# The down projection of the window pairs in seven products of half blocks

## The chip, the cores and the metric

The kernel runs on one core of a Trainium2 chip, in float32. Its time is device microseconds (us) of one execution; the median of several is compared. The engines are TensorE (PE; PEld is its weight load), VectorE (DVE), ScalarE (ACT), GpSimd (POOL) and SyncE (SP); SP and POOL here only issue DMAs.

## The reference

One encoder layer is applied with shared weights to 512 prompt tokens and 2048 sample tokens, model width 1024. The part that matters here is the feed-forward network at its end, with hidden width 2816:

```
h2 = rms(x, norm2_g)
g = silu(dwconv3(h2 @ ffn_w_gate) + bias)     # three taps along the tokens
x = x + (g * (h2 @ ffn_w_up)) @ ffn_w_down
```

Ahead of it stand a norm, an input projection, windowed attention beside a convolution of 31 taps, and an output projection.

## The kernel before, in words

Activations lie transposed, channels on the 128 partitions and tokens along the free axis. Each float32 product is three matmuls of split operands: a high part (ScalarE rounds a copy) and a low part (VectorE subtracts the high part from the raw values) of each operand, high x high, high x low and low x high.

**Slots.** The first part of the kernel is a list of 242 slots (`SLOT`): input projections A of five chunks of 512 tokens (14 slots each), output projections O, and gate, up and down of two plain windows of tokens (G, D). Each slot uses one weight tile of a ring of four, loaded by SP four slots ahead. The input and output projection weights are split once and stored in DRAM (`weight_scratch`); later chunks load them from there. Work of the other engines hangs on the slots in lists (`ACT_SIDE`, `DVE_SIDE`, `POOL_SIDE`), in the engine's own order. A table of room per slot (`ROOM`, `WORK`, `conv_room`) deals VectorE's convolution steps over the slots; the attention part loads `cat` tiles for each O phase.

**Products.** The rest of the tokens is done in two pairs of windows of 414 columns each, in a list of products `PROD`. A gate or up tile pair (two hidden tiles, a "row pair", 11 of them) times two windows is a 2 x 2 block product, computed with seven products (P1 to P7) of half blocks in place of eight: sums of weight quarters (S1 to S4, `part_sum`, line 1907) times sums of window quarters (T1 to T4). A group is one such seven: gate and up of a row pair are two groups. Each product is 4 x 3 = 12 matmuls (line 2354) and needs its weight part split by ScalarE (`part_high`, line 1447) and VectorE (`part_low`, line 1924), three products ahead (`LEAD`), with a ring of four high parts (`HI_RING`).

ScalarE copies three of the seven results out of PSUM, VectorE adds the others to them (`pair_add`), ScalarE and VectorE do the three taps and the swish, VectorE multiplies gate and up (`pair_product`), and the result is split into `mid2` (`pair_mid_high`, line 1520, `pair_mid_low`, line 1980).

**Down.** The down projection of the pairs isn't done by sevens: for each pass (`PASSES`: row pair 0 alone, then five passes of two row pairs) its products D (`pair_down`, line 2358) stand in `PROD` in one run behind one product of the next group, and after the last group of a pair. A D product uses one weight tile for both windows: 24 matmuls. Each of a pass's 16 outputs (8 tiles of model width x 2 windows) is copied from one of four PSUM banks into one of four `pair_y` buffers by ScalarE (`pair_y_copy`, line 1502), and POOL issues a DMA that adds it into `y` in DRAM (line 1176), where the residual already lies. ScalarE waits for a buffer's DMA before it writes it again, and TensorE waits for the copy before it writes the bank again. The weight tiles have a ring of four of their own (`DOWN_RING`), so in a run of D products the split is made one product ahead.

**Order.** For each index of `PROD` each engine has a list (`ACT_AT`, `DVE_AT`, `SP_AT`); an engine works its lists strictly in order and waits on semaphores. The windows of the second pair are loaded, summed and split in the last seven products ahead of it (`WINDOW_STEPS`).

## Time and profile before

| | us |
|---|---|
| median of 3 runs | 2594.53 (2594.07 to 2597.62) |
| profiled execution | 2595.2 |
| its span, first to last instruction | 2592.9 |
| TensorE busy | 2562.3 |
| VectorE busy | 1756.2 |
| ScalarE busy | 1338.4 |
| mean busy share of the DMA engines at 1485 to 2587 us (the pairs) | 0.48 |

The slots take the first 1485 us, the pairs the rest, with 5808 matmuls. Busy time counts matmuls whose modelled spans overlap; the pitch from one to the next is shorter than the duration of one. Shares of DMA are means over the 16 engines; the packets of two queues can overlap on one engine.

### The profile page before, as it was taken

To read this page: it belongs to the slowest core of one execution; us is meant where nothing else is said; L and a number is where in the kernel's file an instruction comes from. 1 tells how busy PE (TensorE), PEld (TensorE's weight loads), DVE (VectorE), ACT (ScalarE), POOL (GpSimd) and SP (SyncE) were. 2 spreads that over 40 slices of the span, in tenths; PEclk is the share of its full clock that TensorE was granted. 3 is DMA by queue.
4 is the path that set the end of the run, shared out by engine and by line. 5 is a ranking of instruction groups with operands and counts; after the bars stand their busy time and mean duration, and the time that the engine had idled before them with its cause. 6 is when DMAs were issued, how large, how long until landed. Compare 5 with 4: busy or idle time off the path is not lost. (4 is left out here: it accounts for less than half of the span.)

```text
span 2592.9 us, 35676 instructions
## 1 busy us (share of the span) xinstructions
PE 2562.3 (99%) x12927; PEld 2288.2 (88%) x12927; DVE 1756.2 (68%) x2908; ACT 1338.4 (52%) x2358; POOL 344.4 (13%) x500
## 2 busy tenths in 40 slices
PE   8999999999999999999999999999999999999998
PEld 6877777788878888888788999999999999999998
DVE  4766658887887697868883666547548754754753
ACT  6345444468337834683573455445445554544543
POOL 0110021101011111110101110120120122012012
PEclk9999999999999999999999999999999999999999
DMA  9967788734554375447439553562554555255254
GB/s 352 343 236 239 249 290 339 276 113 162 209 207 143 138 257 202 169 155 267 156 114 359 189 116 85 109 117 68 116 110 126 115 110 114 72 112 114 67 108 69
DMA packets 161214, 446.76 MB, mean 172 GB/s; under 512 B 27824, under 2 KB 60976, under 8 KB 144400
## 3 DMA queue, kind: packets, MB, share of 16 engines
q1 hardware_dynamic: 108208, 307.75, 34.3%
q0 software_dynamic: 52832, 136.72, 21.6%
q8 instruction: 104, 1.70, 0.3%
q14 instruction: 70, 0.57, 0.1%
HBM read 321.23 MB, written 123.17 MB: 171 GB/s over the span
## 5 line engine op out<-in xcount | busy, mean ns | idle before, releaser
L1930 DVE TENSOR_TENSOR part_lo<-part_raw,part_hi 128x512 fp32r<-128x512 f32 x396 | 271.2, 689 | 425.9 <-ACT part_hi L1462 421.8
L2208 PE MATMUL bank<-hw_hi,weights 128*128 128x462 f32 (+3 forms) x1408 | 420.6, 373 | 0.0
L1751 DVE SCALAR_TENSOR_TENSOR cc<-win,par,cc 128x512 f32<-128x512 f32 x600 | 408.2, 744 | 0.0
L2368 PE MATMUL bank<-mid,part_hi 128*128 128x414 f32 x1408 | 378.4, 349 | 6.9 <-ACT pair_y L1513 4.7
L2159 PE MATMUL bank<-h_hi,weights 128*128 128x512 f32 x1104 | 354.4, 394 | 0.0
L2208 PEld LDWEIGHTS bank<-hw_hi,weights 128*128 128x128 f32 x1408 | 264.7, 188 | 37.3 <-issue 12.2
L1176 POOL DMA_DIRECT2D y_t<-pair_y x192 | 163.4, 861 | 938.9 <-ACT pair_y L1513 936.6
L1462 ACT ACTIVATE part_hi<-part_raw 128x512 fp32r<-128x512 f32 x396 | 244.5, 624 | 81.7 <-PE bank L2354 81.6
L2368 PEld LDWEIGHTS bank<-mid,part_hi 128*128 128x128 f32 x1408 | 262.8, 188 | 12.1 <-ACT pair_y L1513 6.5
L2208 PE MATMUL bank<-hw_lo,weights 128*128 128x464 f32 (+3 forms) x704 | 259.2, 368 | 0.0
L2159 PEld LDWEIGHTS bank<-h_hi,weights 128*128 128x128 f32 x1104 | 207.2, 188 | 51.4 <-issue 5.9
L2354 PE MATMUL bank<-T_hi,part_hi 128*128 128x414 f32 (+1 forms) x704 | 246.2, 350 | 0.2 <-DVE e L1954 0.2
L2354 PE MATMUL bank<-T_lo,part_hi 128*128 128x414 f32 (+1 forms) x704 | 246.1, 350 | 0.0
L2354 PE MATMUL bank<-T_hi,part_lo 128*128 128x414 f32 (+1 forms) x704 | 245.8, 349 | 0.0
L2368 PE MATMUL bank<-mid,part_lo 128*128 128x414 f32 x704 | 245.1, 348 | 0.0
L1513 ACT ACTIVATE pair_y<-bank 128x414 f32<-128x414 f32 x192 | 99.2, 518 | 247.0 <-PE bank L2368 223.6
L1644 DVE TENSOR_TENSOR weights<-wraw,weights 128x1024 fp32r<-128x1024 f32 x154 | 187.9, 1220 | 55.3 <-ACT weights L1198 55.2
L2224 PE MATMUL bank<-mid,weights 128*128 128x462 f32 (+1 forms) x1056 | 223.9, 370 | 0.0
L2224 PEld LDWEIGHTS bank<-mid,weights 128*128 128x128 f32 x1056 | 197.0, 188 | 22.8 <-issue 5.0
L2159 PE MATMUL bank<-h_lo,weights 128*128 128x512 f32 x552 | 215.3, 390 | 0.0
L1198 ACT ACTIVATE weights<-wraw 128x1024 fp32r<-128x1024 f32 x154 | 162.9, 1058 | 91.7 <-DMA wraw<-w_down_t 65.7
L2193 PE MATMUL bank<-cat_hi,weights 128*128 128x512 f32 x640 | 205.2, 395 | 3.0 <-DMA cat_lo<-cat_scratch 3.0
(223 smaller groups left out, 4464.3 us busy)
## 6 DMA issues: line engine op xcount, KB each, us to landing
weights<-weight_scratch SPq DMA_DIRECT2D x88, 1024.0 KB, 6.5
wraw<-w_ffn_t SPq DMA_DIRECT2D x88, 512.0 KB, 3.5
part_raw<-w_ffn_t SPq DMA_DIRECT2D x176, 256.0 KB, 2.7
y_t<-pair_y POOLq DMA_DIRECT2D x192, 207.0 KB, 4.0
weight_scratch<-weights POOLq DMA_DIRECT2D x22, 1024.0 KB, 7.8
wraw<-w_down_t SPq DMA_DIRECT2D x44, 512.0 KB, 3.5
part_raw<-w_pass_t SPq DMA_DIRECT2D x88, 256.0 KB, 3.5
cat_hi<-cat_scratch SPq DMA_DIRECT2D x10, 1024.0 KB, 6.8
```

What stands on the lines that cost most here:

```text
L1176: pool.dma_start(y[o, :, window_start(w):window_start(w) + TP], y_out[n % 4][:], accum_op=ALU.add).then_inc(s_yadd[n % 4], 16)
L1198: nc.scalar.activation(whi[n % RING], wraw[n % RING][:], ACT.Copy).then_inc(s_whi, 1)
L1462: nc.scalar.activation(p_hi[k % HI_RING][:], p_raw[part_of(k)][:], ACT.Copy).then_inc(s_whi, 1)
L1644: nc.vector.tensor_tensor(wlo[n % RING], wraw[n % RING][:], whi[n % RING].bitcast(F32), ALU.subtract) \
L1751: nc.vector.scalar_tensor_tensor(acc, win[i][:, tap:tap + TB], w_tap, acc, ALU.mult, ALU.add).then_inc(s_cv, 1)
L1930: nc.vector.tensor_tensor(p_lo[part_of(k)][:], p_raw[part_of(k)][:], p_hi[k % HI_RING][:].bitcast(F32), ALU.subtract).then_inc(s_wlo, 1)
L2159: mm = nc.tensor.matmul(out[:], l[:, k, :], r[:, k, :], start=(k == 0 and i == 0), stop=(k == KT - 1 and i == 2))
L2193: mm = nc.tensor.matmul(out[:], l[:, k, :], r[:, k, :], start=(k == 0 and i == 0), stop=(k == KT - 1 and i == 2))
L2208: mm = nc.tensor.matmul(out, l[:, k, :], r[:, k, cols], start=(k == 0 and j == 0), stop=(k == KT - 1 and j == 2))
L2224: mm = nc.tensor.matmul(out, l[:, q, :], mid[:, k, part, 0:WIDTH[w]], start=(k == 0 and j == 0), stop=(k == FH - 1 and j == 2))
L2354: mm = nc.tensor.matmul(out, l[:, t, :], r[:, t, cols], start=(p in (1, 2, 5) and t == 0 and j == 0), stop=(t == KH - 1 and j == 2), skip_ ...
L2368: mm = nc.tensor.matmul(bank[BANK_Y[n % 4]][:, 0:TP], l[:, (deep * o + t) % KH, :], mid2[:, t, part, i, :], start=(t == 0 and z == 0), sto ...
```

## The change

- The down projection of the pairs becomes seven products too. A D product is now (pair, pass, product p, row pair): 4 outputs x 3 = 12 matmuls on one part of 256 KB. A pass has 7 phases, in the order 5, 3, 1, 6, 7, 4, 2; a phase has one D product per row pair of the pass. Phases 5, 1 and 2 begin their four banks anew, the others go on in what stands there, so that each phase leaves four results that belong to one of the four quarters of `y` (`DOWN_OUT`); they are copied and added into `y` after every phase, 28 per pass. The ring of `pair_y` buffers has six in place of four.
- Phases of a pass are dealt one by one behind the products of the next row pair, from P6 of its gate group to P4 in its up group. The last pass of a pair stays in one run behind the last group. The changed order of the last group (6, 2, 7, 3) goes.
- `mid2` holds seven tiles (B11, T1, T2, B21, B22, T3, T4) for two row pairs. VectorE makes four sums per row pair (`pair_mid_sum`), and seven tiles are split in place of four.
- The sums of down weights are made in the slots: at slots 12, 17, ..., 62 SP loads the four quarters of a row pair (1 MB), three slots later VectorE makes four sums, and one slot after that POOL stores all four tiles of 256 KB in DRAM (`down_sums`). The load of the next waits for the store of the last. `WORK` knows them, so the convolution steps are dealt anew.
- Some semaphores are shared by more loads (`residual_loaded`, `y_residual_loaded`), and tiles of the pairs lie elsewhere in SBUF.

The core of the diff:

```diff
+COMBO_AT = [12 + 5 * r for r in range(FT // 2)]
...
+for _r in range(FT // 2):
+    DVE_SIDE[COMBO_AT[_r] + 3].append(("combo", _r))
+    POOL_SIDE[COMBO_AT[_r] + 4].append(("combo", _r))
...
+DOWN_ORDER = (5, 3, 1, 6, 7, 4, 2)
+DOWN_FRESH = (5, 1, 2)
+DOWN_OUT = {1: (0, 0), 2: (0, 0), 3: (0, 1), 6: (0, 1), 5: (1, 1), 7: (1, 1), 4: (1, 0)}
+COMBO = {"A21": 0, "A22": 1, "A11": 2, "A12": 3, "S3": 0, "S1": 1, "S2": 2, "S4": 3}
+COMBO_SUMS = (("S1", "A21", "A22"), ("S3", "A21", "A11"), ("S2", "S1", "A11"), ("S4", "A12", "S2"))
...
 PROD = []
 for _q in range(PAIRS):
+    _behind = []
     for _i in range(ROW_PAIRS):
+        if _i > 0 and PASS_OF[_i] != PASS_OF[_i - 1]:
+            _behind = [[("D", _q, PASS_OF[_i - 1], _p, _r) for _r in PASSES[PASS_OF[_i - 1]]] for _p in DOWN_ORDER]
         for _s in range(2):
             _g = 2 * _i + _s
-            PROD += [("P", _q, _g, 1), ("P", _q, _g, 5)]
-            if _g > 0:
-                PROD.append(("P", _q, _g - 1, 4))
-            for _p in (6, 2, 7, 3) if ends_pair(_g) else (6, 2, 3, 7):
-                PROD.append(("P", _q, _g, _p))
-                if _s == 0 and _i > 0 and PASS_OF[_i] != PASS_OF[_i - 1] and _p == DOWN_BEHIND[min(PASS_OF[_i - 1], 1)]:
-                    PROD += [("D", _q, PASS_OF[_i - 1], _j) for _j in range(down_parts(PASS_OF[_i - 1]))]
+            for _p in (1, 5) + (4,) * (_g > 0) + (6, 2, 3, 7):
+                PROD.append(("P", _q, _g - (_p == 4), _p))
+                if _behind and (_s == 1 or _p not in (1, 5, 4)):
+                    PROD += _behind.pop(0)
     PROD.append(("P", _q, GROUPS - 1, 4))
-    PROD += [("D", _q, len(PASSES) - 1, _j) for _j in range(down_parts(len(PASSES) - 1))]
+    PROD += [("D", _q, len(PASSES) - 1, _p, _r) for _p in DOWN_ORDER for _r in PASSES[-1]]
 PRODS = len(PROD)
 
-Y_PAIR = 2 * KT * len(PASSES) * PAIRS
+Y_PAIR = KH * len(DOWN_ORDER) * len(PASSES) * PAIRS
+Y_RING = 6
...
+MID_HIGHS = ("B11", "T1", "B22", "T2", "T3", "B21", "T4")
+MID_LOWS = ("B11", "T1", "B22", "T3", "T2", "B21", "T4")
+MID_SUMS = {"T1": ("B12", "B11"), "T2": ("B22", "T1"), "T3": ("B12", "B22"), "T4": ("B21", "T2")}
+MID_TILE = {"B11": 0, "B12": 1, "B22": 2, "B21": 3}
+V_READ = (2, 4, 5, 7)
...
-    _t = max(_t, _k - (1 if PROD[_k][0] == "D" and PROD[_k][3] >= DOWN_RING else LEAD))
+    _t = max(_t, _k - LEAD)
+    if _k in DOWN_AT and DOWN_AT[_k] >= DOWN_RING:
+        _t = max(_t, min(DOWNS[DOWN_AT[_k] - DOWN_RING] + 3, _k - 1))
...
-        elif _x < 3 or not ends_pass(_gi):
+        else:
             DVE_AT[_t].append(("product", _gi, _x))
-            ACT_AT[_t].append(("mid_high", _gi, _x))
+            if _x != 1:
+                ACT_AT[_t].append(("mid_high", _gi, ("B11", None, "B22", "B21")[_x]))
+            for _b in ((), ("T1",), ("T2", "T3"), ("T4",))[_x]:
+                DVE_AT[_t].append(("mid_sum", _gi, _b))
+                ACT_AT[_t + 1].append(("mid_high", _gi, _b))
...
+            for _i, _b in enumerate((("B11",), (), ("T1", "B22", "T3"), ("T2", "B21", "T4"))[_x]):
+                DVE_AT[_t + 1 + _i // 2].append(("mid_low", _gi, _b))
...
 for _k in DOWNS:
-    ACT_AT[_k + 1].insert(0, ("y_copy", _k))
+    if PROD[_k][4] == PASSES[PROD[_k][2]][-1]:
+        ACT_AT[_k + 1].insert(0, ("y_copy", _k))
...
-                sp.dma_start(p_raw["D", d % DOWN_RING][:], w_pass[d % (len(DOWNS) // PAIRS)]).then_inc(s_rw[d % DOWN_RING], 16)
+                if d == 0:
+                    sp.wait_ge(s_cst, 16 * ROW_PAIRS)
+                p, i = PROD[DOWNS[d]][3:]
+                src = combo_d if A_OF[p] in SUM_ORDER else w_pass
+                sp.dma_start(p_raw["D", d % DOWN_RING][:], src[i, :, COMBO[A_OF[p]]]).then_inc(s_rw[d % DOWN_RING], 16)
+
+            def load_combo(r):
+                if r > 0:
+                    sp.wait_ge(s_cst, 16 * r)
+                sp.dma_start(combo[:], w_pass[r]).then_inc(s_cl, 16)
...
+            def store_combo(r):
+                pool.wait_ge(s_cs, 4 * (r + 1))
+                pool.dma_start(combo_d[r], combo[:]).then_inc(s_cst, 16)
...
-                for n, o, i in y_outputs(k):
-                    add_pair_y(PROD[k][1], n, o, i)
+                q, F, p, r = PROD[k][1:]
+                if r == PASSES[F][-1]:
+                    for n, o in y_outputs(k):
+                        add_pair_y(q, n, KH * DOWN_OUT[p][0] + o, DOWN_OUT[p][1])
...
             def pair_y_copy(k):
-                for z, (n, o, i) in enumerate(y_outputs(k)):
-                    if z == len(y_outputs(k)) - 1:
+                for n, o in y_outputs(k):
+                    if o == KH - 1:
                         act.wait_ge(s_used, SLOTS + k + 1)
                     else:
-                        act.wait_ge(s_dn, DN_PLAIN + n + 1 - DOWN_AT[k])
-                    if n >= 4:
-                        act.wait_ge(s_yadd[n % 4], 16 * (n // 4))
+                        act.wait_ge(s_dn, DN_PLAIN + (KH - 1) * (n // KH) + o + 1)
+                    if n >= Y_RING:
+                        act.wait_ge(s_yadd[n % Y_RING], 16 * (n // Y_RING))
                     elif n == 0:
                         for o_ in range(KT):
                             act.wait_ge(s_yst[o_], 16 * PLAIN)
-                    nc.scalar.activation(y_out[n % 4][:], bank[BANK_Y[n % 4]][:, 0:TP], ACT.Copy).then_inc(s_y, 1)
+                    nc.scalar.activation(y_out[n % Y_RING][:], bank[BANK_Y[o]][:, 0:TP], ACT.Copy).then_inc(s_y, 1)
...
+            def pair_mid_sum(gi, t):
                 u = hidden_pair(gi)
-                i = u % ROW_PAIRS
-                row, w = ROW_WINDOW[x]
-                f = 2 * (i - PASSES[PASS_OF[i]][0]) + row
-                dve.wait_ge(s_mhi, H_PLAIN + 4 * u + seat(gi, x))
-                nc.vector.tensor_tensor(mid2[:, f, 1, w, :], v_buf[x][:], mid2[:, f, 0, w, :].bitcast(F32), ALU.subtract) \
-                  .then_inc(s_mlo, 1)
+                seat_ = mid_seat(u % ROW_PAIRS)
+                before = mid_reader(u, t)
+                if before is not None:
+                    dve.wait_ge(s_used, SLOTS + before + 1)
+                two = []
+                for b in MID_SUMS[t]:
+                    if b in MID_TILE:
+                        dve.wait_ge(s_m, H_PLAIN + 4 * u + MID_TILE[b] + 1)
+                        two.append(v_buf[MID_TILE[b]][:])
+                    else:
+                        dve.wait_ge(s_ms, 4 * u + int(b[1]))
+                        two.append(mid2_raw[:, seat_, B_ORDER.index(b)])
+                nc.vector.tensor_tensor(mid2_raw[:, seat_, B_ORDER.index(t)], two[0], two[1], ALU.subtract).then_inc(s_ms, 1)
+
+            def pair_mid_low(gi, b):
+                u = hidden_pair(gi)
+                seat_ = mid_seat(u % ROW_PAIRS)
+                dve.wait_ge(s_mhi, H_PLAIN + 7 * u + MID_HIGHS.index(b) + 1)
+                if b == "T1" or b == "T2":
+                    dve.wait_ge(s_ms, 4 * u + 2 * int(b[1]))
+                src = v_buf[MID_TILE[b]][:] if b in MID_TILE else mid2_raw[:, seat_, B_ORDER.index(b)]
+                nc.vector.tensor_tensor(mid2[:, seat_, B_ORDER.index(b), 1], src,
+                                        mid2[:, seat_, B_ORDER.index(b), 0].bitcast(F32), ALU.subtract).then_inc(s_mlo, 1)
+
+            def combo_sums(r):
+                dve.wait_ge(s_cl, 16 * (r + 1))
+                for z, (t, a, b) in enumerate(COMBO_SUMS):
+                    if z > 1:
+                        dve.wait_ge(s_cs, 4 * r + z)
+                    nc.vector.tensor_tensor(combo[:, COMBO[t]], combo[:, COMBO[a]], combo[:, COMBO[b]],
+                                            ALU.add if t == "S1" else ALU.subtract).then_inc(s_cs, 1)
...
+            def pair_down(k, q, F, p, i):
+                u, t = ROW_PAIRS * q + i, B_ORDER.index(B_OF[p])
+                phase = down_phase(q, F, p)
                 pe.wait_ge(s_wlo, SPLITS[-1] + k + 1)
-                deep = 2 * len(PASSES[F])
...
+                first, last = i == PASSES[F][0], i == PASSES[F][-1]
+                for o in range(KH):
+                    if first and phase > 0:
+                        pe.wait_ge(s_y, Y_PLAIN + KH * (phase - 1) + o + 1)
+                    for z, (l, part) in enumerate(((a, 0), (a, 1), (b, 0))):
+                        mm = nc.tensor.matmul(bank[BANK_Y[o]][:, 0:TP], l[:, o, :], mid2[:, mid_seat(i), t, part],
+                                              start=(first and p in DOWN_FRESH and z == 0), stop=(last and z == 2),
+                                              skip_group_check=(p not in DOWN_FRESH))
...
+    b = i["ffn_w_down"][0].reshape(ROW_PAIRS, 2, P, 2, KH, P)
+    w_pass = np.stack([b[:, 0, :, 1], b[:, 1, :, 1], b[:, 0, :, 0], b[:, 1, :, 0]], 2)
```

## Rows read from the trace of the kernel before

**Rows 1.** The page's part 1: busy time, share of span, instructions
```profile
PE 2562.3 (99%) x12927; PEld 2288.2 (88%) x12927; DVE 1756.2 (68%) x2908; ACT 1338.4 (52%) x2358; POOL 344.4 (13%) x500
```

**Rows 2.** TensorE's waits, whole span: us in total, times, longest
```profile
PE bank L2368 <- ACT pair_y L1513: 4.7, 6, 2.6
PE bank L2193 <- DMA cat_lo<-cat_scratch: 3.0, 2, 2.1
PE bank L2368 <- DVE mid L1986: 2.0, 4, 1.0
```

**Rows 3.** Windows, matmuls of line 2368 alone: PE busy, PEld busy, clock, DMA
```profile
2150.00:2300.00 150.00, 72.01 (x384) 71.69 (x384) 1.00 0.55 108
```

**Rows 4.** Timeline of VectorE, row pair without down products: start, duration
```profile
1673.93 0.59 DVE L1986 TENSOR_TENSOR mid<-v,mid 128x414 fp32r<-128x414 f32 x1
1674.43 0.69 DVE L1921 TENSOR_TENSOR part_raw<-part_raw 128x512 f32<-128x512 f32 x1
1675.04 0.68 DVE L1930 TENSOR_TENSOR part_lo<-part_raw,part_hi 128x512 fp32r<-128x512 f32 x1
...
1682.93 0.64 DVE L1963 SCALAR_TENSOR_TENSOR v<-e,par,v 128x414 f32<-128x414 f32 x1
...
1684.18 0.58 DVE L1954 TENSOR_TENSOR e<-bank,e 128x416 f32<-128x416 f32 x1
...
2015.48 1.89 DVE L1947 TENSOR_TENSOR T_lo<-T_raw,T_hi 128x1664 fp32r<-128x1664 f32 x1
2017.28 1.89 DVE L1942 TENSOR_TENSOR T_raw<-T_raw,B_raw 128x1664 f32<-128x1664 f32 x1
```

**Rows 5.** Group by line and shape, 1550 us to the end: busy, mean ns
```profile
L1462 ACT ACTIVATE part_hi<-part_raw 128x512 fp32r<-128x512 f32 x371 | 229.6, 625 | 80.8 <-PE bank L2354 80.7
```

**Rows 6.** Timeline, first pass of each pair: copies on ScalarE, issues on POOL
```profile
1532.51 1.31 ACT L1513 ACTIVATE pair_y<-bank 128x414 f32<-128x414 f32 x3
1538.50 0.52 ACT L1513 ACTIVATE pair_y<-bank 128x414 f32<-128x414 f32 x1 [2.87 <-DMA y_t<-pair_y]
...
1555.09 0.52 ACT L1513 ACTIVATE pair_y<-bank 128x414 f32<-128x414 f32 x1 [2.03 <-DMA y_t<-pair_y]
2080.30 0.50 ACT L1513 ACTIVATE pair_y<-bank 128x414 f32<-128x414 f32 x1
...
2103.39 0.52 ACT L1513 ACTIVATE pair_y<-bank 128x414 f32<-128x414 f32 x1 [0.80 <-DMA y_t<-pair_y]
2099.70 0.84 POOL L1176 DMA_DIRECT2D y_t<-pair_y  x1 [3.10 <-ACT pair_y L1513]
2100.76 0.85 POOL L1176 DMA_DIRECT2D y_t<-pair_y  x1 [0.22 <-issue]
```

**Rows 7.** DMA queues, 1536 to 1556 us (q0 adds): packets, MB, share
```profile
q0 software_dynamic: 1904, 2.82, 96.3%
q1 hardware_dynamic: 486, 0.86, 12.6%
```

**Rows 8.** DMA and last copy, 2555 to 2590 us (last pass): median us to landing
```profile
q0 software_dynamic: 2228, 3.29, 77.6%
q1 hardware_dynamic: 576, 1.05, 8.5%
y_t<-pair_y POOLq DMA_DIRECT2D x16, 207.0 KB, 3.8
part_raw<-w_pass_t SPq DMA_DIRECT2D x4, 256.0 KB, 3.4
2586.63 0.52 ACT L1513 ACTIVATE pair_y<-bank 128x414 f32<-128x414 f32 x1 [1.73 <-PE bank L2368]
```

**Rows 9.** Windows: busy of PE, PEld, DVE, ACT, POOL, clock, DMA share, GB/s
```profile
400.00:410.00 10.00, 7.89 (x34) 6.26 (x33) 6.92 (x12) 3.70 (x9) 0.54 (x1) 0.98 0.98 360
```

**Rows 10.** TensorE's longest wait in the pairs, and the window behind it
```profile
2099.46 1.06 PE L2368 MATMUL bank<-mid,part_hi 128*128 128x414 f32 x2 [2.56 <-ACT pair_y L1513]
2098.00:2104.00 6.00, 4.54 (x17) 4.42 (x18) 0.69 (x1) 3.20 (x7) 3.40 (x4) 0.72 0.95 141
```

More of the change, by code:

```diff
@@ L688, in encoder_layer @@
         v_buf = [run(o, (f"v{i}", [P, TP], F32))[0] for i, o in enumerate(v_at)]
[L689 to L690 removed]
+        mid2 = run(m_at, ("mid2", [P, 2, 7, 2, P_PITCH], F32R))[0][:, :, :, :, 0:TP]
+        mid2_raw = run(m_at, ("mid2_raw", [P, 2, 7, 2, P_PITCH], F32))[0][:, :, :, 1, 0:TP]
+        y_out = [run(o, (f"pair_y{i}", [P, TP], F32))[0] for i, o in enumerate(y_at)]
         def part_key(gi, a):
@@ L1900, in y_add @@
                 if h == 0:
[L1901 removed]
+                    dve.wait_ge(s_yl[o // 4], 64 * (w + 1))
                 else:
@@ L2356, in pair_product @@
                 mm.then_inc(s_used, 1)
-            def pair_down(k, q, F, j):
+            def pair_down(k, q, F, p, i):
+                u, t = ROW_PAIRS * q + i, B_ORDER.index(B_OF[p])
+                phase = down_phase(q, F, p)
                 pe.wait_ge(s_wlo, SPLITS[-1] + k + 1)
-                deep = 2 * len(PASSES[F])
-                u = ROW_PAIRS * q + PASSES[F][-1]
+                pe.wait_ge(s_mlo, H_PLAIN + 7 * u + MID_LOWS.index(B_OF[p]) + 1)
                 a, b = p_hi[k % HI_RING], p_lo[part_of(k)]
-                outputs = y_outputs(k)
-                def products(n, o, i, rows):
-                    for t in rows:
-                        for z, (l, part) in enumerate(((a, 0), (a, 1), (b, 0))):
-                            mm = nc.tensor.matmul(bank[BANK_Y[n % 4]][:, 0:TP], l[:, (deep * o + t) % KH, :],
-                                                  mid2[:, t, part, i, :], start=(t == 0 and z == 0),
-                                                  stop=(t == deep - 1 and z == 2))
-                    return mm
-                ahead = deep - 2 if j == 0 else 0
-                if ahead > 0:
-                    pe.wait_ge(s_mlo, H_PLAIN + 4 * u)
-                    for n, o, i in outputs:
-                        if n >= 4:
-                            pe.wait_ge(s_y, Y_PLAIN + n - 3)
-                        products(n, o, i, range(ahead))
-                for n, o, i in outputs:
-                    if j == 0:
-                        pe.wait_ge(s_mlo, H_PLAIN + 4 * u + (3 if i == 1 else 4))
-                    if n >= 4 and ahead == 0:
-                        pe.wait_ge(s_y, Y_PLAIN + n - 3)
-                    mm = products(n, o, i, range(ahead, deep))
-                    if (n, o, i) != outputs[-1]:
@@ new lines, in pair_down @@
+                first, last = i == PASSES[F][0], i == PASSES[F][-1]
[6 more added lines that the diff above has]
+                                              skip_group_check=(p not in DOWN_FRESH))
+                    if last and o < KH - 1:
```

138 lines of the change are left out of this document (74 added, 64 removed).

## The prediction, made before the changed kernel ran

> **What bounds the kernel now.** I read the engine rows of the page first: TensorE is busy 99% of the span, VectorE 68% [rows 1]. Then TensorE's waits over the whole execution: the largest on the down projection of the pairs is 4.7 us for ScalarE's `pair_y` copies, 2.0 us are for `mid`, and 3.0 us elsewhere are for `cat_lo` [rows 2]. So the count of matmuls sets the time, and one matmul of 414 columns is worth its pitch, not its 349 ns: 384 of them fill 72.01 us of a stretch, 0.1875 us each [rows 3]. Then I looked at what the change loads more heavily, VectorE [rows 4, 5] and the DMAs that add `pair_y` into `y` [rows 6 to 8].
>
> **What it removes.** Per row pair (two hidden tiles, two windows) the down projection is 8 outputs x 2 rows x 2 windows x 3 = 96 matmuls; after, 7 products x 4 outputs x 3 = 84. Over 22 row pairs 2112 become 1848: 264 x 0.1875 = **49.5 us**, all on the path.
>
> **What it adds.** (a) `pair_y` outputs: 2 pairs x 6 passes x 16 = 192 become 2 x 6 x 28 = 336, each with a copy, a POOL issue and an adding DMA of 207 KB. (b) Weight tiles of the down products: 88 of 24 matmuls become 154 of 12 (2.25 us), each with a 256 KB load, a high and a low part. (c) Four sums and three low parts more per row pair on VectorE. (d) Eleven loads and eleven stores of 1 MB and 44 sums early on.
>
> **The price of (a).** What matters is the pace at which adding DMAs finish when they queue. The trace shows it in the first pass of each pair, where 16 outputs come in four tiles: copies from 1532.51 to 1555.09 and from 2080.30 to 2103.39, so 15 steps in 22.6 and 23.1 us, 1.51 and 1.54 us each, with a ring of four buffers [rows 6]. In 20 us of the first of these the adding queue's packets fill 96.3% of the 16 engines and the load queue's 12.6%: together over 100%, so they overlap partly [rows 7]. Lower bound: POOL issues one each 1.06 us (2099.70 to 2100.76) [rows 6]. Upper bound, by the calm last pass: 77.6% of 35 us for 16, 1.70 us, and half a load more (8.5% of 35 us for four is 0.74 us each), 2.07 us if nothing overlaps [rows 8]. I take 1.50: the nearest rows are at 1.51 to 1.54, a ring of six should shave a little, more loads give it back. Call it x. From the first copy to a free buffer it is 5.9 us (1532.51 to 1538.50) [rows 6], so copy number n (from 0) can start 5.9 + x(n-6) us after the first.
>
> *First pass, dealt.* Seven down tiles among seven others, 14 x 2.25 = 31.5 us. Without waits copy 27 starts 6 x 4.5 + 1.7 = 28.7 us after the first (the four outputs of a phase lie 3 matmuls apart); it can start at 5.9 + 21 x 1.5 = 37.4. TensorE notices a late copy after some 3.4 us (the next phase is a foreign product away): 8.7 - 3.4 = 5.3 us, twice 10.6. The 4.7 us of before go: **+5.9**.
>
> *Two-row passes, dealt* (4 per pair). A phase takes three tiles, 6.75 us, for four outputs: 1.69 us each, above x. Nothing.
>
> *End of pair 0.* Fourteen down tiles in a row: four outputs per 4.5 us. The last phase starts when copy 23 has freed its bank: 5.9 + 17 x 1.5 = 31.4 against 22.5 + 1.7 = 24.2, 7.2 us late. Here there is next to no slack: the high part of the tile after next stands behind the four copies on ScalarE, 0.52 + 0.62 and VectorE's 0.68 us [rows 4 to 6] of the 2.25. VectorE meanwhile does the next pair's windows, timed in products: 10 sums and low parts at a pitch of 1.80 us and 7 low parts at 0.61 in the seven products before it, 22.3 us [rows 4]; these products took 31.5 us and now 15.75, 6.5 us too little. The two overlap; I take 7.2 + 2, less 1.3 of such waits before: **+7.9**.
>
> *End of pair 1.* Without waits 31.5 us of matmuls, and 6.1 from about their end to the end of the span, 2592.9 (the last copy starts at 2586.63 [rows 8], when they have ended): 37.6. With them: first copy 2.9 us after the first down matmul, then 5.9 + 27x = 46.4, together 49.3: **+11.7**.
>
> **(b)** A load lands in 3.4 us when calm [rows 8]; the ring of four gives 3 x 2.25 = 6.75 us for landing, high and low (1.30). Dealt, it is hidden; in a row it fits barely and lies under the waits above. Without that cover it would be some 0.5 us per tile, 7 us per end. Nothing.
>
> **(c)** Pitches from starts on VectorE: mid low 0.50, weight sum 0.61, two taps 1.25 [rows 4]; a low part is as large as a sum, product and add are as mid low. A row pair without down tiles is 22 x 0.61 + 6 x 0.5 + 4 x 1.25 + 8 x 0.5 = 25.4 us of its 168 x 0.1875 = 31.5; with seven of 0.5 more 28.9. It fits at 92%, in bursts: a low part is asked for three products ahead, so some 5 us of lateness are free. I take **+2** for all 12 such row pairs; the bounds are 0 and 3.5 us each (all the new work on the path).
>
> **(d)** DMA is busy 0.98 at 400 to 410 us [rows 9], where `cat_lo` is already late by up to 2.1 us [rows 2]; no other load is among TensorE's waits, and weights are loaded four slots ahead, which hides most of the new traffic. One 1 MB load and store come in between just ahead of the `cat` loads: **+2.5**, between 0 and 7. VectorE's sums are 4 x 0.6 us per five slots, no matter.
>
> **Clock.** After the wait of 2.56 us at 2099.46 the granted clock of 2098 to 2104 is 0.72: half speed, 1.2 GHz, for part of it, (1 - 0.72) x 6 = 1.7 us [rows 10]. It happened once in the pairs; I count one episode more, **+1.7**.
>
> **Sum.** -49.5 + 5.9 + 7.9 + 11.7 + 2 + 2.5 + 1.7 = -17.8. The profiled execution took 2595.2 us (span 2592.9); it stands 0.7 above the median 2594.5. 2594.5 - 17.8 = **2577 us**.
>
> **Rivals.**
> 1. *Nothing queues.* At x = 1.06 the first passes have no lateness (-4.7), the end of pair 0 costs VectorE's 6.5 - 1.3 = 5.2, the end of pair 1 a few issues of POOL in a row, 1.6, the half clock goes (-1.7), early and VectorE's terms 0: -49.5 + 0.4, 2545 us. For it: low latency when calm, 3.8 us [rows 8], and two more buffers. Against: the engines' share in [rows 7]. Chance 0.18.
> 2. *Slower: the engines' time adds up.* The three terms of (a) together are 86x - 103.5, and with the other 6.2 they eat the 49.5 from x = 1.71 on. If packets of the two queues don't overlap, an adding DMA is 1.45 us (96.3% of 20 us for 13.3 of them [rows 7]) and its share of loads 0.37 at the ends and 0.29 in the first pass: x = 1.82 and 1.74, 44 x 1.82 + 42 x 1.74 - 103.5 + 6.2 = 55.9, 6.4 slower: 2601 us. For it: twice the loads per output time. Against: the sum of 109%. Chance 0.15. The Trainium skill (Trainium Kernel Development and Optimization, Key Constraints) says that DMAs from the SP, ACT and POOL queues all run on the same 16 engines and interleave; by that rule this rival is the forecast, and the trace agrees as far as the engines' share is full, not as to the sum.
> 3. *VectorE becomes the bound* in the row pairs without down tiles. If the queue's idle gaps stay and the 3.5 us come on top, 12 x 3.5 = 42 in place of 2: 2617 us. For it: 92%, and strict order. Against: before, the low parts come 5 us early. Chance 0.10.
> My forecast holds 0.57.
>
> **Range and chances.** All costs at their low ends give 2545, x = 1.8 with the upper part of the early and VectorE's terms 2606; 2551 to 2604 leaves out 2 in 10. 0.2% is 5.2 us, about what a measurement can tell. Faster by more: 0.57 x 0.96 + 0.18 + 0.15 x 0.15 + 0.10 x 0.25 = 0.77; slower: 0.15 x 0.6 + 0.10 x 0.7 = 0.16; within 0.07.
>
> **What would show it.** 1848 matmuls on the down line at an unchanged pitch. In the first pass and at both ends: ScalarE's copies waiting for `y_t`, 1.5 us apart, adding DMAs landing in 6 to 9 us, and TensorE waiting for `pair_y` and for parts some 25 us in all. Between them TensorE without gaps. VectorE above 85% in row pairs without down tiles and TensorE not waiting for it. A longer `cat_lo` wait near 409 us. Wrong it would be by copies 1.2 us apart (faster) or above 1.7 us (slower), or by waits on VectorE's `part_lo`, `e` or `mid` spread over all row pairs.

## The result, and the profile after

Before: 2593.28 us median of 20 executions (2587.86 to 2597.62). After: 2600.42 us median of 20 (2596.34 to 2603.29). The ratio is 1.0025, 95% interval [1.0018, 1.0032]: slower by 7.1 us, where I forecast 2577 us and faster. The time lies in my range, on the wrong side of before.

The profiled execution of after took 2596.34 us (span 2594.6), the lowest of its 20. So the two traces differ by 1.7 us of span only; the other 5.4 us of the medians are not in them.

Part 1 of the page of after, then its rows for the adding DMAs and the copies ahead of them (parts 5 and 6), to stand beside [rows 1] and [rows 8]:

```profile
PE 2525.8 (97%) x12663; PEld 2240.1 (86%) x12663; DVE 1909.2 (74%) x3172; ACT 1455.4 (56%) x2634; POOL 478.2 (18%) x655
...
L1563 ACT ACTIVATE pair_y<-bank 128x414 f32<-128x414 f32 x336 | 159.8, 515 | 63.7 <-DMA y_t<-pair_y 51.9
...
y_t<-pair_y POOLq DMA_DIRECT2D x336, 207.0 KB, 7.0
```

264 matmuls fewer and TensorE 2 points less busy: the work went, and idle time came in its place. TensorE's waits over the whole span (us in total, times, longest), against [rows 2]:

```profile
PE bank L2453 <- ACT pair_y L1563: 19.1, 22, 3.3
PE bank L2438 <- DVE e L2009: 10.0, 8, 3.2
PE bank L2263 <- ACT weights L1248: 7.9, 1, 7.9
PE bank L2355 <- DVE qk L1770: 7.2, 1, 7.2
PE bank L2453 <- DVE part_lo L1985: 3.9, 9, 0.7
PE bank L2277 <- DMA cat_lo<-cat_scratch: 3.5, 2, 2.6
PE bank L2368 <- DVE row_max L1866: 2.3, 1, 2.3
```

The wait for `weights` is the start of the kernel. `e` (10.0) was 0.2 before and `qk` (7.2) was 0.5, `row_max` (2.3) is new, and `pair_y` grew from 4.7 to 19.1.

**Where the time went.** I took the start of every matmul of the pairs and set the time from each product to the next against its matmuls at 0.1875 us. What is over is lost there, half clock included. Before, the pairs took 1100.3 us for 5808 matmuls (1089.0), 11.4 lost; after, 1089.9 us for 5544 (1039.5), 50.3 lost. In us, pair 0 and pair 1:

| place | before | after | difference | my term |
|---|---|---|---|---|
| 264 matmuls | | | -49.5 | -49.5 |
| pairs' first matmul starts at | 1485.9 | 1495.7 | +9.8 | +2.5 |
| first passes (groups 2 and 3) | 4.3, 5.3 | 10.5, 7.2 | +8.1 | +5.9 |
| groups 4 to 6 | 0 | 2.0, 2.5 | +4.5 | +2 (VectorE) |
| last group, P7 to P4 | 0 | 5.4, 2.8 | +8.2 | none |
| end of pair 0 | 1.7 | 12.2 | +10.5 | +7.9 |
| end of pair 1 and after its last matmul | 1.1 + 6.7 | 8.0 + 9.0 | +9.2 | +11.7 |
| clock | | inside the rows above | | +1.7 |

Together +0.8; places under 0.4 us and rounding make the rest of 1.7.

*The copies.* ScalarE, first pass of pair 0 and last pass of pair 1 (start, duration), against [rows 6, 8]:

```profile
1539.69 1.72 ACT L1563 ACTIVATE pair_y<-bank 128x414 f32<-128x414 f32 x4
...
1577.79 0.52 ACT L1563 ACTIVATE pair_y<-bank 128x414 f32<-128x414 f32 x1 [0.70 <-DMA y_t<-pair_y]
...
2550.53 2.20 ACT L1563 ACTIVATE pair_y<-bank 128x414 f32<-128x414 f32 x4 [0.90 <-PE bank L2453]
...
2585.41 1.08 ACT L1563 ACTIVATE pair_y<-bank 128x414 f32<-128x414 f32 x2
```

Copy 27 starts 38.1 us after copy 0 in the first pass of pair 0 (I had 37.4) and 35.4 in the last pass of pair 1. From the seventh copy on they are 1.56 and 1.49 us apart in the first passes, 1.69 and 1.42 at the ends.

*DMA in the last pass*, 2550 to 2586 us (queues: packets, MB, share of the 16 engines; then median us to landing), against [rows 7, 8]:

```profile
q0 software_dynamic: 3366, 4.97, 82.7%
q1 hardware_dynamic: 1412, 2.56, 22.5%
...
y_t<-pair_y POOLq DMA_DIRECT2D x26, 207.0 KB, 7.1
part_raw<-w_pass_t SPq DMA_DIRECT2D x5, 256.0 KB, 6.0
part_raw<-down_sums SPq DMA_DIRECT2D x4, 256.0 KB, 6.2
```

Again 105% together: the engines are full, and an adding DMA lands in 7.1 us instead of 3.8.

*P7 to P4 in the last group.* VectorE behind P7, whose last matmul starts at 1994.15; then TensorE's P4, and the window behind it (us, PE busy, clock, DMA share, GB/s), against [rows 10]:

```profile
1994.68 0.69 DVE L1985 TENSOR_TENSOR part_lo<-part_raw,part_hi 128x512 fp32r<-128x512 f32 x1 [1.17 <-ACT part_hi L1514]
1995.29 0.58 DVE L2033 TENSOR_TENSOR v<-e,v 128x414 f32<-128x414 f32 x1
1995.96 0.59 DVE L2049 TENSOR_TENSOR mid_raw<-v,v 128x414 f32<-128x414 f32 x1
1996.47 0.58 DVE L2058 TENSOR_TENSOR mid<-v,mid 128x414 fp32r<-128x414 f32 x1
1996.97 0.58 DVE L2009 TENSOR_TENSOR e<-bank,e 128x414 f32<-128x414 f32 x1
...
1997.70 0.68 PE L2438 MATMUL bank<-T_hi,part_hi 128*128 128x414 f32 x1 [3.20 <-DVE e L2009]
...
1996.00:2004.00 8.00, 6.30 (x19) 0.57 0.54 187
```

P4 needs `e`, to which P7's result is added. In every other group P1 and P5 of the next lie between; in the last group the change left nothing between, and VectorE has four operations queued ahead of the add. The granted clock then falls to 0.57 over 8 us: half speed for 6.8 us.

*End of pair 0.* VectorE, ScalarE, TensorE:

```profile
2029.99 1.89 DVE L1997 TENSOR_TENSOR T_raw<-B_raw,T_raw 128x1664 f32<-128x1664 f32 x1
...
2031.97 1.59 ACT L1527 ACTIVATE T_hi<-T_raw 128x1664 fp32r<-128x1664 f32 x1 [2.42 <-DVE T_raw L1997]
2033.47 1.31 ACT L1563 ACTIVATE pair_y<-bank 128x414 f32<-128x414 f32 x3
...
2034.11 0.76 PE L2453 MATMUL bank<-mid,part_hi 128*128 128x414 f32 x2 [3.26 <-ACT pair_y L1563]
```

The longest wait for `pair_y` is not a late DMA: ScalarE waits 2.42 us for VectorE's window sum and then rounds the window, with its copies queued behind it.

*The slots.* VectorE and TensorE near 380 us, then median us to landing for DMAs issued from 340 to 375 us:

```profile
376.12 0.69 DVE L1855 TENSOR_TENSOR qt_lo<-qt,qt_hi 128x512 fp32r<-128x512 f32 x1 [12.04 <-ACT kw_hi L1355]
...
377.47 2.74 DVE L2066 TENSOR_TENSOR combo<-combo 128x512 f32<-128x512 f32 x4
...
380.72 0.74 DVE L1770 SCALAR_TENSOR_TENSOR qk<-qk,qg,bank 128x512 f32<-128x512 f32 x1
...
381.61 0.77 PE L2355 MATMUL bank<-q_parts,spread 128*128 128x512 f32 x1 [7.25 <-DVE qk L1770]
...
combo<-w_pass_t SPq DMA_DIRECT2D x1, 1024.0 KB, 8.9
...
cat_scratch<-ln_st POOLq DMA_DIRECT2D x2, 256.0 KB, 9.7
kw<-k_scratch POOLq DMA_DIRECT2D x1, 320.0 KB, 12.1
```

In before `ln_st` and `kw` land in 7.8 and 10.7 us, and the same two operations of VectorE and TensorE are these:

```profile
373.44 0.69 DVE L1800 TENSOR_TENSOR qt_lo<-qt,qt_hi 128x512 fp32r<-128x512 f32 x1 [7.90 <-ACT kw_hi L1305]
...
376.27 0.47 PE L2271 MATMUL bank<-q_parts,spread 128*128 128x512 f32 x1 [0.45 <-DVE qk L1715]
```

The chain behind it, from the landings and the timelines of both traces: a store of `ln_st` issued near 353 us lands 2.1 us later than in before (360.98 against 358.88), ScalarE's `ln_acc` starts as it lands (361.00 against 358.90), POOL issues the load of `kw` 1.2 us later behind that, and `kw` itself takes 1.4 us longer. `qt_lo` is 2.7 us late, and the four sums ahead of `qk` make 2.7 more. The clock is at half from 379.0 to 385.8 us, 4.2 us of it behind the end of TensorE's wait, worth 2.1.

Matmul by matmul (the 7119 ahead of the pairs have the same order in both) the 9.8 us are: -1.5 up to here, most of it a wait of 1.27 us for `t_rs` near 51 us that after does not have; +6.8 at this wait; +2.1 by its half clock; and +2.4 near 537 us, where TensorE waits 2.3 us for `row_max`. Ahead of that `row_max` VectorE waits 1.49 us for ScalarE; what made it late was not tested.

### The profile page after: what moved, and what is told of

Same layout as the page of the kernel before. It is cut to its first block and busy times, and to the rows that moved or that the text cites. A ratio compares the mean times of both kernels' runs of the same rounds, so it can differ in the third digit from the quotient of the medians.

```text
span 2594.6 us, 36381 instructions
## 1 busy us (share of the span) xinstructions
PE 2525.8 (97%) x12663; PEld 2240.1 (86%) x12663; DVE 1909.2 (74%) x3172; ACT 1455.4 (56%) x2634; POOL 478.2 (18%) x655
## 5 line engine op out<-in xcount | busy, mean ns | idle before, releaser
L1985 DVE TENSOR_TENSOR part_lo<-part_raw,part_hi 128x512 fp32r<-128x512 f32 x462 | 317.2, 689 | 293.9 <-ACT part_hi L1514 290.6
L1224 POOL DMA_DIRECT2D y_t<-pair_y x336 | 291.6, 1213 | 801.1 <-ACT pair_y L1563 799.3
L2453 PE MATMUL bank<-mid,part_hi 128*128 128x414 f32 x1232 | 335.2, 353 | 24.5 <-ACT pair_y L1563 19.1
L1514 ACT ACTIVATE part_hi<-part_raw 128x512 fp32r<-128x512 f32 x462 | 284.7, 627 | 131.8 <-PE bank L2438 52.3
L2292 PEld LDWEIGHTS bank<-hw_hi,weights 128*128 128x128 f32 x1408 | 264.7, 188 | 37.3 <-issue 12.2
L2453 PEld LDWEIGHTS bank<-mid,part_hi 128*128 128x128 f32 x1232 | 229.0, 189 | 38.2 <-ACT pair_y L1563 15.8
L2453 PE MATMUL bank<-mid,part_lo 128*128 128x414 f32 x616 | 215.2, 349 | 0.0
L1563 ACT ACTIVATE pair_y<-bank 128x414 f32<-128x414 f32 x336 | 159.8, 515 | 63.7 <-DMA y_t<-pair_y 51.9
```

Source lines behind the costliest of these rows:

```text
L1224: pool.dma_start(y[o, :, window_start(w):window_start(w) + TP], y_out[n % Y_RING][:], accum_op=ALU.add).then_inc(s_yadd[n % Y_RING], 16)
L1514: nc.scalar.activation(p_hi[k % HI_RING][:], p_raw[part_of(k)][:], ACT.Copy).then_inc(s_whi, 1)
L1985: nc.vector.tensor_tensor(p_lo[part_of(k)][:], p_raw[part_of(k)][:], p_hi[k % HI_RING][:].bitcast(F32), ALU.subtract).then_inc(s_wlo, 1)
L2292: mm = nc.tensor.matmul(out, l[:, k, :], r[:, k, cols], start=(k == 0 and j == 0), stop=(k == KT - 1 and j == 2))
L2453: mm = nc.tensor.matmul(bank[BANK_Y[o]][:, 0:TP], l[:, o, :], mid2[:, mid_seat(i), t, part], start=(first and p in DOWN_FRESH and z == 0), ...
```

## The experiments

Each ran in 5 rounds beside the kernel before, 4 to 11 executions of each. The last column is against the changed kernel, (ratio - 1.0025) x 2593.3 us, and uncertain by some 3 us, 4 where only 4 or 5 executions stand; expectations count from its median, 2600.4.

| kernel | median us | ratio [95%] | us against after |
|---|---|---|---|
| sums_moved | 2586.7 | 0.9977 [0.9967, 0.9988] | -12.4 |
| down_before_p4 | 2593.7 | 1.0002 [0.9992, 1.0012] | -6.0 |
| sparse_first_pass | 2578.9 | 0.9949 [0.9935, 0.9962] | -19.7 |
| plain_stores | 2571.3 | 0.9916 [0.9902, 0.9929] | -28.3 |
| thin_adds | 2568.5 | 0.9904 [0.9890, 0.9917] | -31.4 |
| windows_earlier | 2597.1 | 1.0017 [1.0006, 1.0027] | -2.1 |
| all_three | 2560.4 | 0.9878 [0.9862, 0.9894] | -38.1 |
| all_four | 2559.6 | 0.9866 [0.9853, 0.9880] | -41.2 |
| end_dealt | 2553.8 | 0.9852 [0.9839, 0.9866] | -44.9 |
| ring5 | 2617.2 | 1.0092 [1.0078, 1.0106] | +17.4 |
| sums_thin_work | 2598.8 | 1.0015 [1.0007, 1.0024] | -2.6 |
| sums_thin_traffic | 2591.2 | 0.9992 [0.9983, 1.0001] | -8.6 |

**sums_moved**: the eleven down sums at other slots.

```
-COMBO_AT = [12 + 5 * r for r in range(FT // 2)]
+COMBO_AT = [12 + 4 * r for r in range(9)] + [64, 69]
```

> The changed kernel with only the slots of the early weight sums moved: 12, 16, ..., 44, then 64 and 69, so that none of their loads and stores falls between slots 48 and 63. Theory A (the 1 MB store and load at slots 51 and 52 delay the load of kw, ScalarE's kw_hi and behind it VectorE, until TensorE waits 7.2 us for qk and then runs 6.8 us at half clock): that wait falls to about 0.5 us as before the change, the first product of the pairs starts 8 to 10 us earlier, near 1486 us in place of 1495.7, and the time is 9 us below the changed kernel, 0.9990 of the kernel before. Rival B (VectorE is late by its own new work, the 44 sums and the convolution steps dealt anew, wherever they stand): the pairs still start at 1493 us or later and the time stays within 3 us of the changed kernel.

The first matmul of the pairs starts at 1485.17 (before 1485.9), and the wait for `qk` is back at 0.4 us. The early loss came from where the sums stood, not from there being sums. The start of the pairs scatters from trace to trace: 1495.3 to 1501.9 us in the seven kernels here that keep the changed kernel's slots as they are (the changed kernel itself 1495.7), 1482.2 to 1486.1 in the four with the sums moved. The loss is in every trace, and 9.8 us is near its low end, which fits the 12.4 us by the medians.

**sums_thin_work and sums_thin_traffic**: which half of them.

```
 sums_thin_work
-nc.vector.tensor_tensor(combo[:, COMBO[t]], combo[:, COMBO[a]], combo[:, COMBO[b]],
+nc.vector.tensor_tensor(combo[:, COMBO[t], 0:1, 0:16], combo[:, COMBO[a], 0:1, 0:16], combo[:, COMBO[b], 0:1, 0:16],
 sums_thin_traffic
+few = slice(0, KH) if r == 0 else slice(0, 1)
-sp.dma_start(combo[:], w_pass[r])
+sp.dma_start(combo[:, :, few], w_pass[r][:, :, few])
...
-pool.dma_start(combo_d[r], combo[:])
+pool.dma_start(combo_d[r][:, :, few], combo[:, :, few])
```

> The changed kernel, its loads and stores of the down sums whole, but each of VectorE's four sums over 16 of 1024 columns (the rest of these sums is left out, so y is not the reference's). The pairs started 9.8 us later than before in the traces, and the run with moved sums gave back 13.7 us. Theory A, VectorE's four sums (2.74 us together) standing ahead of the scores' operations are the delay: 2587 to 2591 us, pairs start below 1489. Theory B, the transfers of 1 MB in and 1 MB out delay the stores and loads that the attention waits for: 2597 us or more, pairs start above 1492. In between if both count.

> The changed kernel with VectorE's sums whole, but all loads and stores of the down sums after the first cut to one of eight blocks of columns (128 KB less seven eighths; the sums left out are replaced by the first row pair's, so y is not the reference's). Theory B, traffic: 2586 to 2591 us, pairs start below 1489, the wait of PE for qk near 381 us falls from 7.2 us to under 3. Theory A, VectorE's work: 2597 us or more, that wait stays above 5 us.

Two sizes in these texts are wrong: a sum has 512 columns, not 1024, and the tile has four blocks of columns, not eight, so a cut transfer is 256 KB instead of 1024. TensorE's wait for `qk` and its first matmul in the pairs, thin work and then thin traffic:

```profile
PE bank L2355 <- DVE qk L1770: 5.4, 1, 5.4
...
1494.82 0.42 PE L2438 MATMUL bank<-B_hi,part_hi 128*128 128x416 f32 x1 [1.36 <-DVE yb L1960]
```

```profile
PE bank L2357 <- DVE qk L1772: 1.8, 1, 1.8
...
1489.33 0.43 PE L2440 MATMUL bank<-B_hi,part_hi 128*128 128x416 f32 x1 [1.36 <-DVE yb L1962]
```

It is mostly the transfers. From 340 to 375 us thin traffic has the landings of `ln_st` at 6.9 us, `kw` at 9.0 and `attn_hi` at 6.4, where the changed kernel has 9.7, 12.1 and 11.6 and thin work 9.7, 12.3 and 11.6. TensorE's wait for `qk` falls from 7.2 to 5.4 us without VectorE's sums and to 1.8 us without most of the traffic, of which a quarter stayed. The times fall by 2.6 us, which the intervals don't tell from nothing, and by 8.6. The starts of the pairs, 0.9 and 6.4 us earlier, say less, since each trace has a stall elsewhere too: thin work a wait of 2.0 us near 220 us, thin traffic the one for `row_max`, 2.3 us near 529 us, each with 3.4 us at half clock. The first run lies within the limits of theory B, the second just outside (2591.2 against 2591, 1489.3 against 1489).

**down_before_p4**: one half product of the last pass between P7 and P4.

```
-    PROD.append(("P", _q, GROUPS - 1, 4))
-    PROD += [("D", _q, len(PASSES) - 1, _p, _r) for _p in DOWN_ORDER for _r in PASSES[-1]]
+    _last = [("D", _q, len(PASSES) - 1, _p, _r) for _p in DOWN_ORDER for _r in PASSES[-1]]
+    PROD += _last[:1] + [("P", _q, GROUPS - 1, 4)] + _last[1:]
```

> The changed kernel with the first down product of the last pass put between P7 and P4 of the last group of each pair. Theory A (P4 of the last group waits for VectorE's add of P7's result because nothing lies between them any more; 3.2 and 2.6 us, then 6.8 us at half clock for pair 0): 2.25 us of each wait go and the half clock at 1997 us with it, in all 5 to 8 us below the changed kernel, 0.9998 of the kernel before. Rival B (the run of down products behind it is bound by its adding DMAs and takes the time back): less than 2 us below the changed kernel.

What the last groups lose falls from 5.4 and 2.8 to 1.1 and 1.1 us, the sum of waits for `e` from 10.0 to 4.6. The half clock near 1997 is gone as well, so laying 2.25 us of work into a wait of 3.2 us saves more than 2.25: 4.3 us at the end of pair 0.

**sparse_first_pass**: the single row pair's seven phases behind every second product, spread over 14 products instead of 7. Its `mid` moves to the other seat, since row pair 1 would overwrite the first.

```
+            if _i == 1:
+                _behind = [_x for _d in _behind for _x in (_d, [])]
...
-    return i - PASSES[PASS_OF[i]][0]
+    return 1 if i == 0 else i - PASSES[PASS_OF[i]][0]
```

> The changed kernel with the seven phases of the first pass of each pair dealt behind every second product in place of every one (row pair 0 keeps the other seat of mid2, so that its tiles stay until row pair 2). Four outputs then come per 6.75 us in place of 4.5. Theory A (the adding DMAs need 1.3 to 1.4 us each and set the time of the first pass): TensorE's waits for pair_y between 1540 and 1580 and between 2090 and 2120 us go, 17.7 us lost there become less than 3, and the time is 12 to 16 us below the changed kernel, 0.9970 of the kernel before. Rival B (the waits come from ScalarE's order, copies behind other work, not from the pace of the DMAs): at least half of the loss stays.

```profile
PE bank L2455 <- ACT pair_y L1565: 7.0, 8, 3.3
PE bank L2440 <- DVE e L2011: 6.7, 3, 3.2
```

The first passes lose 1.2 us instead of 17.7, and groups 4 to 6 1.2 instead of 4.5: those waits for `e` were what the first pass left behind, not a load of their own. It is the largest gain of the schedule edits and leaves no work out. Whether the DMAs or ScalarE's order made the loss it does not tell, since it relieves both; the next two runs do.

**plain_stores and thin_adds**: what makes these DMAs slow. The first leaves the addition out (they overwrite `y`), the second all but 16 of 414 columns.

```
 plain_stores
-pool.dma_start(y[...], y_out[n % Y_RING][:], accum_op=ALU.add)
+pool.dma_start(y[...], y_out[n % Y_RING][:])
 thin_adds
-pool.dma_start(y[o, :, window_start(w):window_start(w) + TP], y_out[n % Y_RING][:],
+pool.dma_start(y[o, :, window_start(w):window_start(w) + 16], y_out[n % Y_RING][:, 0:16],
```

> The changed kernel with the pair_y DMAs as plain stores to the same places, with nothing added (so y of the pairs is not the sum): same bytes, same issues, no read of y. Theory A (it is the adding that makes these DMAs slow, 1.3 to 1.4 us each when they queue): plain ones of 1656 bytes per partition take under 0.8 us of the engines, no copy waits for its buffer, and the first pass, both ends of pairs and the tail give back 30 us or more: 2566 us, 0.989 of the kernel before. Rival B (POOL's issue at 1.06 us and the number of DMAs are what counts): less than 12 us below the changed kernel.

> The changed kernel with every adding DMA cut to the first 16 of its 414 columns (the other columns of these outputs are left out); the number of DMAs, their issue and the ring of six stay. Theory A, the bytes that are read, added and written set the pace: with a twenty-sixth of them nothing is lost in the first passes and at the ends but what plain stores of full length lost too, 2571 us or less, ratio 0.992 or less. Theory B, a fixed cost per adding DMA or per row of it sets the pace: the first passes lose what they lost, 2590 us or more.

The last pass of plain_stores (2536 to 2566 us), then of thin_adds (2530 to 2560 us), same view as for after:

```profile
q0 software_dynamic: 1536, 5.09, 44.7%
...
y_t<-pair_y POOLq DMA_DIRECT2D x26, 207.0 KB, 4.3
```

```profile
q0 software_dynamic: 3469, 0.20, 34.4%
...
y_t<-pair_y POOLq DMA_DIRECT2D x27, 8.0 KB, 3.3
```

5 MB added take 3366 packets and 82.7% of 36 us; 5 MB stored take 1536 packets and 44.7% of 30 us. Per tile of 0.212 MB that is 29.8 / 23.4 = 1.27 us of all engines against 13.4 / 24.0 = 0.56. So adding costs 2.3 times a plain store. With thin adds it is 34.4% of 30 us for 27, 0.38 us each: some of the cost is there for hardly any bytes. The end of pair 1 loses 2.0 us without the addition and 1.1 with thin adds, instead of 8.0: there the bytes added are nearly the whole cause, and POOL, which issues as many in thin_adds, is not one.

The first passes keep 7.5 and 7.4 of their 17.7 us, which is not the DMAs' doing. ScalarE in the first pass of pair 0 of plain_stores:

```profile
1555.10 0.64 ACT L1548 ACTIVATE v<-e,par 128x414 f32<-128x414 f32 x1 [1.99 <-DVE e L2008]
...
1556.18 1.71 ACT L1562 ACTIVATE pair_y<-bank 128x414 f32<-128x414 f32 x4
```

No copy waits for its buffer here; the four stand in ScalarE's list behind `v`, which waits for VectorE's `e`, and TensorE waits 1.08 us for the first of them. So rival B of sparse_first_pass has a share, at most the 42% that stay, and theory A the rest.

The end of pair 0 keeps 8.2 and 7.1 of 12.2, so most of that has another cause: the wait of 3.26 us for `pair_y` at 2034 us, behind the rounding of the window, is there with 3.25 and 3.12 us too.

The Trainium skill (DMA: Bandwidth & Descriptors, Rules for kernel authors) says that an accumulate reads its destination and writes it later; twice the packets for the same bytes agree with it.

**windows_earlier**: pair 1's window work begun 12 products ahead instead of 7.

```
-WINDOW_STEPS = [(-7, "sum T1"), (-6, "low B11"), (-6, "sum T2"), (-5, "low T1"), (-5, "sum T3"), (-4, "sum T4"), ...
+WINDOW_STEPS = [(-12, "sum T1"), (-10, "low B11"), (-10, "sum T2"), (-8, "low T1"), (-8, "sum T3"), (-7, "sum T4"), ...
+WINDOW_HIGHS = (-12, -10, -8, -6, -5, -3, -1)
...
-            ACT_AT[_n - 7 + _i].append(("window_high", _q, _b))
+            ACT_AT[_n + WINDOW_HIGHS[_i]].append(("window_high", _q, _b))
```

> The changed kernel with the window work of pair 1 (seven roundings on ScalarE, eleven operations of 1.88 us on VectorE) begun 12 products before pair 1 instead of 7, since a product between the pairs is now 12 matmuls long instead of 24. Theory A: at least half of the 12.2 us lost at the end of pair 0 is that these steps are timed in products and now have half the time: the loss there falls to 6 us or less and the kernel takes 2593 to 2596 us, ratio 0.9985 to 1.001. Theory B: the adding DMAs set the pace of the last pass there (28 copies, 1.3 us each, against 31.5 us of matmuls) and the window work only sits beside it: 2599 to 2602 us, no change, and the loss stays above 10 us.

TensorE's waits from 1995 to 2045 us:

```profile
PE bank L2454 <- DVE part_lo L1986: 4.6, 5, 1.7
...
PE bank L2454 <- ACT pair_y L1564: 0.2, 1, 0.2
```

The end of pair 0 loses 8.8 instead of 12.2, neither 6 nor more than 10. The `pair_y` waits are gone there (after: 5.2 us in 1990 to 2045), and `part_lo` stands in their place (after: 1.9): the same 20 us of VectorE's window operations now delay the halves. The time is not told from the changed kernel's with certainty, as the intervals overlap.

**all_three and all_four**: sums_moved, down_before_p4 and sparse_first_pass in one kernel; then with windows_earlier.

> The three edits that each took something off alone, in one kernel: sums of down parts at slots 12 to 44, 64 and 69 (alone 13.7 us under the changed kernel), the first half product of the last pass between P7 and P4 of the last group (alone 6.7 us), and the single row's phases behind every second product (alone 21.5 us). Theory A, three separate stalls: the gains add, 2600.4 - 13.7 - 6.7 - 21.5 = 2558.5 us, ratio 0.986 to 0.988; pairs start near 1485, and the end of pair 0 and the end of pair 1 still lose some 12 and 8 us. Theory B, the stalls overlap (what one edit frees is lost at the next wait or at half clock): less than two thirds of the sum, 2572 us or more.

> All three and the earlier window work together. By theory A of the window work 5 to 6 us under the kernel with three edits, some 2553 us, ratio 0.984; by theory B equal to it within 2 us.

The three gains were 12.4 + 6.0 + 19.7 = 38.1 us, and the kernel with all three gained 38.1. With intervals of 3 to 4 us on each, the agreement to a tenth is luck, but two thirds of the sum, theory B, is far off: they are three separate stalls. The fourth edit adds 3.1 us by the ratios and 0.8 by the medians; the intervals overlap, and it is neither the 5 to 6 us of one theory nor surely the nothing of the other.

**end_dealt**: all_four, and the last three phases of pair 0's last pass behind P1, P5 and P6 of pair 1, the window work spread from 6 products ahead to 9 behind.

```
-    _behind = []
+    _behind = _over
...
-                if _behind and (_s == 1 or _p not in (1, 5, 4)):
+                if _behind and (_s == 1 or _p not in (1, 5, 4) or _i == 0):
...
+    if _q + 1 < PAIRS:
+        _over = [_last[8:10], _last[10:12], _last[12:]]
+        _last = _last[:8]
...
+WINDOW_STEPS = [(-6, "sum T1"), (-5, "low B11"), (-4, "sum T2"), (-2, "low T1"), (-1, "sum T3"), (1, "sum T4"),
+                (3, "low T2"), (5, "low B21"), (6, "low B22"), (7, "low T3"), (9, "low T4")]
+WINDOW_HIGHS = (-6, -4, -2, 0, 2, 4, 6)
```

> The kernel with four edits, and the last three of the seven phases of pair 0's last pass behind the first three products (P1, P5, P6) of pair 1 instead of ahead of them; the window work is spread from 6 products before pair 1 to 9 after it. Theory A: what is left at the end of pair 0 (9.7 us there) is two queues in the same 31.5 us, adding DMAs at 1.3 us each and 11 x 1.88 us of window operations ahead of the rounded halves; with products laid between the phases both have room, 6 to 9 us of it go, 2551 to 2554 us, ratio 0.983 to 0.985, and the end of pair 1 still loses 8 us. Theory B: the loss moves with the phases (each of the three waits for its banks or halves among pair 1's products, or the rounding of the window is late for P5 and P6): 2557 us or more.

```profile
PE bank L2460 <- ACT pair_y L1570: 2.7, 6, 0.6
PE bank L2460 <- DVE part_lo L1992: 2.5, 6, 0.4
PE bank L2445 <- DVE e L2016: 2.3, 3, 1.0
```

2553.8 us, by the ratio 38 us below before and the fastest here. The end of pair 0 loses 4.7 instead of 9.7 in all_four, a little less than I expected; the end of pair 1, behind which nothing lies, still 7.4. The mean granted clock is 0.999.

**ring5**: five output tiles instead of six. Seven were not run.

```
-Y_RING = 6
+Y_RING = 5
```

> The changed kernel with five output tiles between ScalarE's copies and the adding DMAs instead of six. Theory A, in the four bursts (two first passes, two ends) the DMAs' pace sets the time and the ring is only what lets the first copies run ahead: one tile less costs one more pace of 1.3 us in each burst, 3 to 7 us in all, 2603 to 2607 us, ratio 1.004 to 1.007; the two-row passes dealt behind groups still lose nothing. Theory B, the latency of 7.0 us sets it, at ring over latency: a copy every 1.4 us with five instead of 1.17 with six, 0.23 us x 28 x 4 = 26 us more, 2620 us or more.

16.8 us more by the medians, and neither theory's figure. The 28 copies take 42.2, 44.1, 41.3 and 37.5 us in the four bursts instead of 38.1, 41.0, 37.4 and 35.4: 3.3 us each, not 1.3 and not 6.3. With fewer in flight each lands sooner (page of ring5):

```profile
L1563 ACT ACTIVATE pair_y<-bank 128x414 f32<-128x414 f32 x336 | 163.7, 515 | 133.7 <-DMA y_t<-pair_y 116.2
...
y_t<-pair_y POOLq DMA_DIRECT2D x336, 207.0 KB, 6.6
```

So neither the engines' time nor the turn-around alone is the pace, and the `y_t` waits of ScalarE double (51.9 to 116.2 us) by one tile. Whether a seventh tile would gain as much is not shown.

## Why the prediction was wrong

1. **The matmuls** (-49.5): right. 264 fewer, at 0.1875 us; the stretches between the places of the table lose nothing.
2. **The step that failed: (d), "+2.5, between 0 and 7".** It was +9.8, and 12.4 by the run with the sums moved. I looked at weights and `cat` near 409 us, where DMA was known to be full, and not at the other chains that go through DRAM in the slots. The wait for `cat_lo` that I priced grew by 0.5 us only. At 345 to 375 us the share is 0.96 in before and 1.00 in after; the stores of `ln_st` and the load of `kw` take 1.9 and 1.4 us longer there, the work behind them is 2.7 us late, and TensorE waits 7.2 us for `qk`. "VectorE's sums are no matter" failed too, but by less: 2.74 us ahead of `qk`, and the run without them is 2.6 us faster, within its interval. 2.4 of the 9.8 us stand at another place, near 537 us, whose cause was not tested.
3. **A wait that I did not see: P7 to P4**, +8.2 by the table, 6.0 by the run. The diff drops the special order 6, 2, 7, 3 of the last group. I costed what was added, moved and removed, but not this order, by which P3 lay between P7 and P4.
4. **(a), the price of the adding DMAs**, 25.5 forecast: 27.8 by the table, and 4.5 more in groups 4 to 6. That the sum is near is in part luck. The pace x = 1.50 held (1.56 and 1.49 in the first passes, 1.42 in the last, but 1.69 at the end of pair 0), and so did the time to copy 27 (37.4 against 38.1 and 37.4). What did not hold is the 3.4 us of slack that I took off per first pass: copies 9.4 and 8.7 us late went with losses of 10.5 and 7.2, so 17.7 in place of 10.6, and 7.5 of these stay when the DMAs are cheap, most of it where ScalarE's copies stand behind work that waits for VectorE, which had no term. Against this I credited 4.7 us for before, where the product starts give 9.6. At the end of pair 0 I had both causes but gave the window work 2 us; it seems the larger one, since 7 to 8 of the 12.2 us stay when the DMAs are cheap, though starting it earlier took off only 3.4. The end of pair 1 was 2.5 us cheaper than I said, by its pace.
5. **(c), VectorE, +2**: the row pairs without down products lose nothing, as the bound of 0 had it. The 4.5 us in groups 4 to 6 are the first pass again, as they go with it.
6. **Clock, +1.7**: too little. Leaving out the very end, before has two stretches at half clock, 3.4 us each at 409.6 and 2099.1; after has four, 6.8 us at 379.0 and 1996.9 and 3.4 at 416.5 and 2034.4. Some 17 us of them lie behind waits, against 6.5 in before, which is an estimated 5 us more. This cost is inside the terms above: 3.0 us beside the wait of 3.20, 1.7 beside that of 3.26.
7. **The rest up to the medians**, 5.4 us, is between executions and not in the two traces: the profiled one of after is 4.1 us below its median, that of before (2595.2) 1.9 above its own. Why executions differ stays open. The clock may have a part: the profiled execution of after has 0.995, the median of its 20 has 0.9935, and 0.0015 x 2600 is 3.9 us. So may the slots: the pairs start at 1495.7 us here, and at 1496.8 in the middle one of the seven traces with the same slots. No trace of a slower execution of the same kernel was compared.

Rival 2 gave 2601 us, nearly the time measured, by a mechanism that did not happen: it needs an adding DMA every 1.74 to 1.82 us, where the bursts had 1.42 to 1.69. What it took from the Trainium skill (Trainium Kernel Development and Optimization, Key Constraints), that the queues share the 16 engines, holds here as far as the share is full; the sum of 82.7% and 22.5% is once more over 100%. Rival 3 did not happen. The signs of my terms were right, but for (c), which was nothing. Two places that cost 7 to 8 us each more than I had, the early sums and P7 to P4, make 15.5 of the 19.5 us between forecast and profile; with one of them mended the kernel took 0.9977 and 1.0002 of the time of before.
